# Gathering an expert's rows to 128 partitions with three of every four used, in a routed-experts layer in float32

## The reference, cut to what matters

```python
def hier_moe(x, ...):                       # x: normalized tokens, 1104 x 1024
    g = argmax(softmax(x @ w_rg + b_rg))    # one of 4 groups
    top_v, top_i = top_k(softmax(le_sel), 2)# two of the group's 8 experts
    expert = g * 8 + top_i                  # 2 of 32 experts for each token
    ...
    h = silu(xb @ w_eg[e]) * (xb @ w_eu[e]) # 1024 -> 512, twice
    return h @ w_ed[e]                      # 512 -> 1024
    ...                                     # times its gate, summed per token
```

## Time and profile before

| what | value |
| --- | --- |
| median of 3 runs | 1085.29 us (1083.37 to 1086.68) |
| the profiled execution's own time | 1084.18 us |
| its span, first to last instruction | 1082.3 us |
| mean granted TensorE clock | 0.974 of full |
| PE busy | 1015.9 us (94%) |
| DVE, ACT, POOL busy | 418.9, 241.0, 108.5 us |
| DMA, whole span | 262.34 MB, mean 242 GB/s |

### The profile page before, as it was taken

How to read it: one execution, slowest core, us unless ns; L and a number is a source line. 1 busy time by engine, 2 the same in 40 slices (tenths; PEclk the granted TensorE clock), 3 DMA queues, 4 the chain that set the end, 5 groups by cost and what they waited for, 6 DMA issues and landing times.

```text
span 1082.3 us, 33080 instructions
## 1 busy us (share of the span) xinstructions
PE 1015.9 (94%) x14746; PEld 827.0 (76%) x14746; DVE 418.9 (39%) x910; ACT 241.0 (22%) x509; POOL 108.5 (10%) x168
## 2 busy tenths in 40 slices
PE   8999999999999999989999999999999999999910
PEld 8786777768685959457888988889888898888810
DVE  2334443535262535362623323233232332323338
ACT  2442232323332322130110111111111111111123
POOL 0110101010100101001010111101111011110000
PEclk9999999999999999999999999999999999999965
DMA  9900010000000000629999999999999999999667
GB/s 331 347 19 40 1 40 0 39 0 39 0 39 20 18 39 1 274 115 332 402 404 398 406 405 399 412 401 406 404 395 408 392 406 394 387 402 384 272 226 297
DMA packets 53075, 262.34 MB, mean 242 GB/s; under 512 B 10301, under 2 KB 12925, under 8 KB 44842
## 3 DMA queue, kind: packets, MB, share of 16 engines
q1 hardware_dynamic: 43274, 234.20, 54.9%
q0 software_dynamic: 7168, 18.10, 5.0%
q10 hardware_dynamic: 2592, 9.44, 2.1%
HBM read 242.00 MB, written 26.80 MB: 248 GB/s over the span
## 4 chain that ended last, share of the span: by engine, by line
PE 91%; DVE 4%; DMA 2%; issue 1%; ACT 1%; SPq 0%; ACTq 0%; POOLq 0%; DVEq 0%
PE bank L1564 32%; PE bank L1279 18%; PE bank L1400 11%; PE bank L1575 10%; PE bank L1331 6%; PE bank L1581 6%; PE bank L1260 4%; DVE arena L1238 1%; PE bank L1380 1%; DVE arena L1236 1%; DVE arena L1244 1%; DMA arena<-in_w_in 1%; PE bank L1338 1%; PE bank L1397 1%; DMA arena<-pick_rows 1%
## 5 line engine op out<-in xcount | busy, mean ns | idle before, releaser
L1279 PE MATMUL bank<-xnT,arena 128*128 128x128 f32 x1728 | 201.0, 277 | 3.1 <-DMA arena<-in_w_in 1.8
L1279 PEld LDWEIGHTS bank<-xnT,arena 128*128 128x128 f32 x1728 | 196.8, 193 | 5.5 <-DVE sA L862 3.5
L1564 PEld LDWEIGHTS bank<-xnT,arena 128*64 128x64 f32 x4096 | 170.4, 137 | 6.5 <-issue 6.2
L1564 PEld LDWEIGHTS bank<-hnT,arena 128*64 128x64 f32 x4096 | 169.6, 137 | 7.5 <-issue 7.5
L1564 PE MATMUL bank<-hnT,arena 128*64 128x96 f32 x4096 | 173.0, 246 | 0.5 <-issue 0.5
L1564 PE MATMUL bank<-xnT,arena 128*64 128x96 f32 x4096 | 173.4, 247 | 0.0
L1120 DVE TENSOR_SCALAR mixT<-mixT 128x384 f32<-128x384 f32 x32 | 11.8, 368 | 319.5 <-ACT mixT L735 319.5
L1400 PE MATMUL bank<-arena,mixT 128*128 128x512 f32 x256 | 111.7, 593 | 0.0
L1400 PEld LDWEIGHTS bank<-arena,mixT 128*128 128x128 f32 x256 | 47.9, 190 | 57.2 <-issue 57.1
L1575 PE MATMUL bank<-arena,silu_r 128*32 128x384 f32 x768 | 85.8, 487 | 0.5 <-issue 0.5
L1581 PE MATMUL bank<-arena,osq 128*32 128x256 f32 x384 | 86.0, 380 | 0.0
(11 more groups left out here) (228 smaller groups left out, 975.1 us busy)
## 6 DMA issues: line engine op xcount, KB each, us to landing
arena<-in_w_eg SPq DMA_DIRECT2D x32, 2048.0 KB, 15.9
arena<-in_w_eu SPq DMA_DIRECT2D x32, 2048.0 KB, 16.3
arena<-in_w_ed SPq DMA_DIRECT2D x32, 2048.0 KB, 16.5
hn_rows<-hs ACTq DMA_DIRECT2D x18, 512.0 KB, 3.3
arena<-pick_rows SPq DMA_DIRECT2D x16, 512.0 KB, 10.8
arena<-in_w_in SPq DMA_DIRECT2D x3, 2048.0 KB, 11.8
arena<-in_w_out SPq DMA_DIRECT2D x1, 4096.0 KB, 13.5
out_y_prompt<-arena SPq DMA_DIRECT2D x8, 512.0 KB
```

The source lines that it names most:

```text
L1279: last = mm(out, w_in_sb[:, k, a:b], xnT[:, k, :], start=k == 0, stop=k == KD - 1)
L1564: last = mm(out[q * SW:(q + 1) * SW, n * BLOCK:(n + 1) * BLOCK], w[:, k, m * P + q * SW:m * P + (q + 1) * SW], rowsT[b][:, k, :], start=k ...
```

## The change

The rows of an expert are gathered to all 128 partitions: 32 groups of four partitions, of which the first three are used (lanes 0, 1, 2 of each group), 96 in all as before. A function `lane_of` gives the group and the lane of each rank: 16 consecutive ranks go to 16 different groups, over a table of two sets of groups. Two tables of ranks stand in the constants: `iota_lane` (128 wide, -1 at an unused lane) and `iota_block` (96 wide, the same ranks without the unused lanes). `at_rank`, `idx_f` and `idx_i` become 128 wide. The turn of the rows gives 128 columns in place of 96, and the copy out of PSUM reads the three used ones of each four, so `rowsT` has 96 columns as before, in the order of `iota_block`. The scatter still has 96 rows and needs an index without the unused lanes: three new DMAs on ScalarE's queue pick them from `idx_i` into `slot_idx`.

```diff
+LANE_GROUP = 4
+LANE_USED = LANE_GROUP * BLOCK // P
+LANE_GROUPS = P // LANE_GROUP
+LANE_SETS = ((0, 3, 5, 6, 9, 10, 12, 15), (1, 2, 4, 7, 8, 11, 13, 14))
+def lane_of(rank):
+    turn, n = divmod(rank, 16)
+    group = 16 * (n // 8) + LANE_SETS[turn % 2][n % 8]
+    return group, turn // 2
...
-    put("iota_block", (SPREAD * (np.arange(BLOCK) % RUN) + np.arange(BLOCK) // RUN)[None, :])
+    for rank in range(BLOCK):
+        group, n = lane_of(rank)
+        of_slot[LANE_USED * group + n] = rank
+        of_lane[LANE_GROUP * group + n] = rank
+    put("iota_block", of_slot[None, :])
+    put("iota_lane", of_lane[None, :])
...
-        at_rank = sb("at_rank", [P, PICKS, BLOCK])
+        at_rank = sb("at_rank", [P, PICKS, P])
-        idx_i = sb("idx_i", [BLOCK, NE], I32)
+        idx_i = sb("idx_i", [P, NE], I32)
+        slot_idx = sb("slot_idx", [BLOCK, NE], I32)
...
-        rows = [spare[0:BLOCK, 0:D], xs[0:BLOCK, :, :].rearrange("p k n -> p (k n)")]
+        rows = [spare[:, 0:D], xs[:, :, :].rearrange("p k n -> p (k n)")]
...
-                nc.gpsimd.tensor_copy(pick_idx[b][:, :], idx_i[:, bass.ds(e, 1)])...
+                nc.gpsimd.tensor_copy(pick_idx[b][:, :], slot_idx[:, bass.ds(e, 1)])...
+            pool.wait_ge(s["slot_idx_in"], 16 * LANE_USED)
             scatter(0, 0, first=True)
...
+            act.wait_ge(s["idx_ready"], 1)
+            for n in range(LANE_USED):
+                act.dma_start(slot_idx[n:BLOCK:LANE_USED, :], idx_i[n:P:LANE_GROUP, :]).then_inc(s["slot_idx_in"], 16)
             act.wait_ge(s["hn_stored"], 16 * PICKS * TILES)
...
-                    rank(V.tensor_scalar(at_rank[:, k, :], con("iota_block"), rk[:, k:k + 1], None, ALU.is_equal))
+                    rank(V.tensor_scalar(at_rank[:, k, :], con("iota_lane"), rk[:, k:k + 1], None, ALU.is_equal))
...
-                    V.tensor_tensor(rowsT[b][:, k, :], bank[half][:, 0:4 * BLOCK].rearrange("p (k n) -> p k n", n=BLOCK),
-                                    g_ffn[:, k].unsqueeze(2).to_broadcast([P, KD // 2, BLOCK]), ALU.mult)...
+                    V.tensor_tensor(rowsT[b][:, k, :].rearrange("p k (g n) -> p k g n", n=LANE_USED),
+                                    bank[half][:, :].rearrange("p (k g n) -> p k g n", g=LANE_GROUPS, n=LANE_GROUP)[:, :, :, 0:LANE_USED],
+                                    g_ffn[:, k].unsqueeze(2).unsqueeze(3).to_broadcast([P, KD // 2, LANE_GROUPS, LANE_USED]), ALU.mult)...
...
-                    last = mm(bank[7][0:BLOCK, 192:192 + NE], at_rank[:, k, :], M_tok[:, k, :], ...)
+                    last = mm(bank[7][:, 192:192 + NE], at_rank[:, k, :], M_tok[:, k, :], ...)
...
-                        last = turn(bank[half][:, k * BLOCK:(k + 1) * BLOCK], rows[b][:, c:c + P], BLOCK)
+                        last = turn(bank[half][:, k * P:(k + 1) * P], rows[b][:, c:c + P], P)
```

More of the change, by code:

```diff
@@ L67 @@
 NO_ROW = 4096
-SPREAD = 16
-RUN = BLOCK // SPREAD
+LANE_GROUP = 4
+LANE_USED = LANE_GROUP * BLOCK // P
+LANE_GROUPS = P // LANE_GROUP
+assert LANE_USED * LANE_GROUPS == BLOCK
+LANE_SETS = ((0, 3, 5, 6, 9, 10, 12, 15), (1, 2, 4, 7, 8, 11, 13, 14))
[3 more added lines that the diff above has]
+    return group, turn // 2
 BIG = 3.0e38
@@ L84 @@
 _WIDTHS = [("ident", P), ("keep", PAIRS * P), ("causal", P), ("before", P), ("count_fix", NG * META),
-           ("iota_block", BLOCK), ("iota_e", NE), ("first_g", GROUPS), ("first_e", PER_GROUP), ("pick", PICKS),
+           ("iota_block", BLOCK), ("iota_lane", P), ("iota_e", NE), ("first_g", GROUPS), ("first_e", PER_GROUP), ("pick", PICKS),
            ("valid", 1), ("block_edge", EXTRA_PER_E), ("iota_x", EXTRA), ("edge_x", EXTRA)]
@@ L107, in constants @@
     put("count_fix", np.concatenate([w / np.minimum(np.arange(META) + 1, w) for w in WINDOWS])[None, :])
-    put("iota_block", (SPREAD * (np.arange(BLOCK) % RUN) + np.arange(BLOCK) // RUN)[None, :])
+    of_slot, of_lane = np.full(BLOCK, -1.0), np.full(P, -1.0)
+    for rank in range(BLOCK):
[4 more added lines that the diff above has]
+    put("iota_lane", of_lane[None, :])
     put("iota_e", np.arange(NE)[None, :])
@@ L273, in build @@
         gate_all = sb("gate_all", [P, TILES, PICKS])
-        idx_f = sb("idx_f", [BLOCK, NE])
-        idx_i = sb("idx_i", [BLOCK, NE], I32)
+        idx_f = sb("idx_f", [P, NE])
+        idx_i = sb("idx_i", [P, NE], I32)
+        slot_idx = sb("slot_idx", [BLOCK, NE], I32)
         NP = TILES * PICKS
@@ L302, in build @@
         assert NH <= 3 * P
-        rows_idx = [sb(f"rows_idx{b}", [BLOCK, 1], I32) for b in range(2)]
+        rows_idx = [sb(f"rows_idx{b}", [P, 1], I32) for b in range(2)]
         pick_idx = [sb(f"pick_idx{b}", [BLOCK, 1], I32) for b in range(2)]
@@ L329, in build @@
             pe_eT pe_g pe_u2 pe_d sig_ready hid_ready eT_ready ye_ready row_idx_ready
-            x_tab_dve x_tab_pe x_idx_ready x_w x_rows x_pe x_dve x_act x_stored x_pool pick_idx_ready
+            x_tab_dve x_tab_pe x_idx_ready x_w x_rows x_pe x_dve x_act x_stored x_pool pick_idx_ready slot_idx_in
             fin_ready frstd_ready g_fin_in""").split()
@@ L509, in scatter @@
                     wait_parted(pool, ye_stored[b], 16 * t, s["parted"])
-                nc.gpsimd.tensor_copy(pick_idx[b][:, :], idx_i[:, bass.ds(e, 1)]).then_inc(s["pick_idx_ready"], 1)
+                nc.gpsimd.tensor_copy(pick_idx[b][:, :], slot_idx[:, bass.ds(e, 1)]).then_inc(s["pick_idx_ready"], 1)
                 wait_parted(pool, s["pick_idx_ready"], e + 1, s["parted"])
@@ L539, in _ @@
                     with pool.If(n < n_x):
-                        nc.gpsimd.tensor_copy(rows_idx[0][:, :], idx_xi[:, bass.ds(n, 1)]).then_inc(s["x_pool"], 1)
+                        nc.gpsimd.tensor_copy(rows_idx[0][0:BLOCK, :], idx_xi[:, bass.ds(n, 1)]).then_inc(s["x_pool"], 1)
                         wait_parted(pool, s["x_pool"], n + 1, s["parted"])
-                        nc.gpsimd.indirect_dma_start(rows[0], None, hn_dram, bass.IndirectOffsetOnAxis(ap=rows_idx[0][:, :], axis=0),
+                        nc.gpsimd.indirect_dma_start(rows[0][0:BLOCK, :], None, hn_dram, bass.IndirectOffsetOnAxis(ap=rows_idx[0][0:BLOCK, :], axis=0),
                                                      bounds_check=PICK_ROWS - 1, oob_is_err=False).then_inc(s["x_rows"], 16)
                         wait_parted(pool, s["x_act"], (1 + YE_STEPS) * (n + 1), s["parted"])
-                        nc.gpsimd.indirect_dma_start(y_dram, bass.IndirectOffsetOnAxis(ap=rows_idx[0][:, :], axis=0), ye[0], None,
+                        nc.gpsimd.indirect_dma_start(y_dram, bass.IndirectOffsetOnAxis(ap=rows_idx[0][0:BLOCK, :], axis=0), ye[0], None,
                                                      bounds_check=PICK_ROWS - 1, oob_is_err=False).then_inc(s["x_stored"], 16)
@@ L1010, in last_rank @@
                 rank.then(V.tensor_reduce(rk[:, :], prod[:, :, :], AX.X, ALU.add))
-                rank(V.tensor_scalar(at_rank[:, 0, :], con("iota_block"), rk[:, 0:1], None, ALU.is_equal))
-                V.tensor_scalar(at_rank[:, 1, :], con("iota_block"), rk[:, 1:2], None, ALU.is_equal).then_inc(s["onehot_ready"], 1)
+                rank(V.tensor_scalar(at_rank[:, 0, :], con("iota_lane"), rk[:, 0:1], None, ALU.is_equal))
+                V.tensor_scalar(at_rank[:, 1, :], con("iota_lane"), rk[:, 1:2], None, ALU.is_equal).then_inc(s["onehot_ready"], 1)
                 rank(V.tensor_tensor(prod_e[:, :, :], Mk, con("iota_e").unsqueeze(1).to_broadcast([P, PICKS, NE]), ALU.mult))
@@ L1019, in back_idx @@
                 rank(V.tensor_scalar(token[:, :], token[:, :], float(P), None, ALU.add))
-                V.tensor_tensor(idx_f[:, :], idx_f[:, :], bank[7][0:BLOCK, 192:192 + NE], ALU.add).then_inc(s["idx_added"], 1)
+                V.tensor_tensor(idx_f[:, :], idx_f[:, :], bank[7][:, 192:192 + NE], ALU.add).then_inc(s["idx_added"], 1)
             def body(i, first=False, last=False, second=False, third=False):
@@ L1096, in _ @@
             dve.wait_ge(s["pe_idx"], TILES)
-            V.tensor_tensor(idx_i[:, :], idx_f[:, :], bank[7][0:BLOCK, 192:192 + NE], ALU.add).then_inc(s["idx_ready"], 1)
+            V.tensor_tensor(idx_i[:, :], idx_f[:, :], bank[7][:, 192:192 + NE], ALU.add).then_inc(s["idx_ready"], 1)
             back_weights(j)
@@ L1112, in rows_turned @@
                     k = slice(half * KD // 2, (half + 1) * KD // 2)
-                    V.tensor_tensor(rowsT[b][:, k, :], bank[half][:, 0:4 * BLOCK].rearrange("p (k n) -> p k n", n=BLOCK),
-                                    g_ffn[:, k].unsqueeze(2).to_broadcast([P, KD // 2, BLOCK]), ALU.mult).then_inc(s["eT_ready"], 1)
+                    V.tensor_tensor(rowsT[b][:, k, :].rearrange("p k (g n) -> p k g n", n=LANE_USED),
+                                    bank[half][:, :].rearrange("p (k g n) -> p k g n", g=LANE_GROUPS, n=LANE_GROUP)[:, :, :, 0:LANE_USED],
```

(9 more changed lines are left out.)

## The result

| | before | after |
| --- | --- | --- |
| median, 10 runs each | 1086.78 us (1083.37 to 1089.32) | 1092.3 us (1089.51 to 1094.53) |
| ratio after to before | | 1.0055 (95%: 1.0042 to 1.0067), +6.0 us |
| span of the profiled execution | 1082.3 us | 1092.4 us |

The change makes the kernel slower by 0.55%, clear of the 0.3% that I had named. The prediction of 1087.1 us was too low, and so was the range, which ended at 1090.8. The profiled execution of before (1084.18 us) was quicker than nine of the ten runs, and that of after (1094.34 us) was the second slowest of ten, so the two spans differ by 10.1 us where the runs differ by 6.

What follows compares the result with a forecast made beforehand. TensorE was taken to bound the kernel, with no DMA in the expert stage's chain. Turn 1.9, marking product 0.3, passage 0.1 + 0.1 made +2.4 us, on 1084.7 giving 1087.1 us; range 1084.0 to 1090.8.

Steps and rivals of the forecast that it cites:

- What bounds the kernel: Expert stage: waits run over TensorE alone, 16.84 us from one up product to the next, no DMA in the chain.
- The turn: Eight transposes per expert, 128 columns for 96: 109 ns each for 101, 0.06 us an expert, +1.9 us; ceiling 7.2.
- rival C: Expert stage: the turn costs per column, 28 ns a transpose, 7.2 us in place of 1.9, total 1092.4 us; chance 0.06.
- The marking product: Front stage, L1449: stationary side grows from 96 to 128 columns, 8 ns a record over 9 tiles, +0.3 us (0 to 1.5).
- The passage: Last ranks to expert 0: wider at_rank +0.1 us; gather +0.1 us, more indices up to +0.4, more partitions down to -0.5.
- The copy, the three DMAs, the new wait, the constants: Expert 0's copy, other experts' covered copies, ScalarE's DMAs, GpSimd's wait and 64 KB more constants: each taken as cost 0.
- The base: Whole kernel before the change: 1084.7 us, the middle of four executions, on which the sum was put.
- Rival A: Late expert stage: empty gather entries put the DMA behind, TensorE waits 3.0 us for weights, total 1090.1 us; chance 0.13.
- Rival B: Expert stage: gathering to 128 partitions relieves the DMA, weights land in 16 us to the end, 1085.8 us; chance 0.17.

Runs made afterwards that it cites:

- The turn done twice: Kernel before, with the 8 transposes of each turn from expert 1 on done twice, the second over the first; ratio 1.0167, +18.1 us.
- the wide turn alone: Kernel before, with only the 128-column turn and a copy reading the first 96 of each 128; gather, ranks and scatter unchanged; ratio 1.0062, median 1091.89 us.
- the turn of 64 rows: Kernel before, with 7 of the 8 transposes of a turn cut to 64 rows and 64 columns; ratio 1.0005 against before.
- the turn of 96: The change, with turn and copy put back to 96 columns, rows on partitions 96 to 127 left out; ratio 0.9992 against before, median 1085.07 us.
- the plain order: The change, with before's order of ranks on the 128 partitions; ratio 1.0064 against before, median 1091.01 us.

## Why the prediction was wrong, step by step

**What bounds the kernel: right.** The chain of waits is TensorE's before and after, the step between experts holds everything, and a change of 0.2 us in it shows in full.

**The turn: mis-sized by 4.8 us (1.9 for 6.7), and the step that failed.** I divided the 0.81 us of a group of 96-column transposes by eight, got 101 ns, and compared it with 109 ns from a group of the front stage. The two groups have different neighbours. Ask for the same records one by one, by windows of 20 ns (each row begins with the start of the earliest transpose in its window). Before, in the expert stage:

```profile
605.94 0.30 PE L1260 MATMUL bank<-cst,xs 96*128 96x96 f32 x1
606.08 0.41 PE L1260 MATMUL bank<-cst,xs 96*128 96x96 f32 x3
606.16 0.41 PE L1260 MATMUL bank<-cst,xs 96*128 96x96 f32 x3
606.25 0.41 PE L1260 MATMUL bank<-cst,xs 96*128 96x96 f32 x3
606.33 0.41 PE L1260 MATMUL bank<-cst,xs 96*128 96x96 f32 x3
...
606.58 0.25 PE L1260 MATMUL bank<-cst,xs 96*128 96x96 f32 x1
606.75 0.52 PE L1575 MATMUL bank<-arena,osq 128*32 128x384 f32 x3
```

From 606.08 to 606.58 there are six steps, 83 ns each. The first takes 0.14 us (605.94 to 606.08) and the last 0.17 us (606.58 to 606.75), which I put down to the array going over from and to matmuls of another size; that reading was not tested by itself. The front stage is in line with it: behind the group of eight in the earlier trace rows stand two more 128 x 128 transposes, of `k_dec`, and from the second of them to the 64 x 64 products that follow, the step is 0.20 us and not 0.11, in all nine tiles. After:

```profile
610.39 0.33 PE L1285 MATMUL bank<-cst,xs 128*128 128x128 f32 x1
610.55 0.38 PE L1285 MATMUL bank<-cst,xs 128*128 128x128 f32 x2
610.66 0.38 PE L1285 MATMUL bank<-cst,xs 128*128 128x128 f32 x2
610.77 0.38 PE L1285 MATMUL bank<-cst,xs 128*128 128x128 f32 x2
...
611.21 0.27 PE L1285 MATMUL bank<-cst,xs 128*128 128x128 f32 x1
611.41 0.52 PE L1600 MATMUL bank<-arena,osq 128*32 128x384 f32 x3
```

110 ns each inside (610.55 to 611.21), with 0.16 and 0.20 us at the ends. The front stage's group has 109 to 110 ns throughout, and full-size instructions stand on both sides of it. So the row that I took was right for the new pace and the row that I held against it was not the old pace: 109 - 83 = 26 ns a transpose, and not 8. The 26 ns are the ceiling that I had worked out (28 ns, 7.2 us) and made rival C at a chance of 0.06. The turn done twice shows the split of pace and ends in its own kernel, the wide turn alone shows the sum. What no run separates is the cause inside a transpose: with its moving columns the partitions that it contracts over grew too, from 96 to 128. The Trainium skill (FP8 and Floating Point Precision, "TensorE Precision Notes") gives true float32 four passes; for 128 columns at 2.4 GHz that makes an estimate of 213 ns, and the trace has 110. So the trace disagrees with four passes for a transpose, and disagreed before; what I drew from that, that columns hardly cost, didn't follow. Two cycles a column at 2.4 GHz, also an estimate, make 107 ns for 128 columns and 80 for 96, each 3 ns under the measured pace; but for 64 columns they make 53 ns, and the turn of 64 rows has 62, so this fits only the upper two.

**The marking product: 0.6 us for 0.3.** 20 ns a record, between my bounds of 0 and 43, in the seven tiles where projections follow it; in the eighth TensorE waits behind it, and the step is 0.95 us before and after. Between the pooling products of the first and the last tile the kernels with before's tables took 397.5 to 397.6 us, those with the change's 398.1 (the turn of 96), 398.6 (the plain order) and 399.2 (the change). The turn of 96 has just the 0.6 us. The other 0.5 and 1.0 us stand in one step, from the pooling product of the third tile to that of the fourth (52.06 and 52.60 us for 51.56); in the change's chain most of it is a pause of 0.69 us at 152.96 us, marked "issue". The turn of 96 has the same tables and no such pause, so it is not shown to be theirs.

**The passage: about 0.5 us the other way.** The gather's step took 3.70, 3.89 and 3.95 us in the three profiled executions with 128 partitions and 4.14 to 4.42 in the six with 96. I had put +0.1 and allowed for -0.5. The issue on GpSimd grew from 1.13 to 1.18 us, not by a third.

**The copy, the three DMAs, the new wait, the constants: right.** The three DMAs are issued from 488.4 to 489.6 us, beside a first gather that lands sooner than before's. The copy's median on `xnT` is 556 ns before and after, though it now reads pieces of three:

```profile
L1137 DVE TENSOR_TENSOR xnT<-bank,g_ffn x32: 545/556/558, 494.3 to 1004.2; 128x384 f32<-128x384 f32 x32
```

**The base.** I put the sum on 1084.7 us, from four executions; ten runs have before at 1086.78. Of the 5.2 us between 1087.1 and the measured 1092.3, 2.1 are this base, and the rest is the change: 5.5 us between the medians, 6.0 by the ratio, for 2.4. The parts are 6.7 us from the turn and 0.6 from the tables, less 0.5 from the passage, 6.8 us on paper; the runs say 6.0 (4.6 to 7.3). The rest of the 10 us between the two profiles is chance as far as can be seen: 0.7 us in the first weights' step (9.68 for 8.96), 0.9 from there to the first tile, with the clock at its lower level for 6.8 us there in place of 3.4, the 1.0 us of the step between two tiles, and 1.1 us in the first up product.

**Rival A: wrong.** The empty entries built no backlog; q0 took 8.0% of the engines with 1478 packets where it had taken 9.6% with 1344. (That an empty entry moves nothing is so by the queue's count of bytes and not by the HBM's, as the last section shows.) **Rival B: half right.** The relief is real and is worth nothing. The Trainium skill's port map (SBUF — State Buffer, "Door 1: The DMA port swizzle") speaks for it, and the weights' landing agrees in its direction: at the same step of TensorE, gate weights land after 10.4 us with 128 partitions and after 14.4 to 15.9 us in three profiles with 96. The gathers themselves land after 10.1 to 12.0 us from 600 us on where before's took 7.9 to 13.3, no quicker on the whole, so which step of the DMA got cheaper is not shown. **Rival C: what happened.**

## What to carry to other kernels

Two groups of the same instruction can be compared only by the steps inside them; the ends of a group belong to its neighbours, and in a group of eight they were 0.3 of 0.8 us. When a bound from another row gives nearly four times the value that you take, look at single records before you give it 6%. And relieving a queue that is full but that nobody waits for gains no time, so it must not cost anything on the engine that sets the pace: here it cost 0.2 us an expert.

## What the runs showed of the hardware

The entries that a gather's bounds check skips are read from HBM all the same, by the count of bytes. The HBM line of the page, of the change and then of the wide turn alone, which gathers as before:

```profile
HBM read 246.26 MB, written 26.80 MB: 250 GB/s over the span
```

```profile
HBM read 242.00 MB, written 26.80 MB: 247 GB/s over the span
```

The change has 32 gathers x 32 more empty entries; at 4096 bytes each that is 4.19 MB, and 0.07 MB are the wider constants (64 KB): together the 4.26 MB of difference. The queue's own count of bytes stays at 18.10 MB in both. Here it cost no time: the turn of 96 has the same 246.26 MB and before's time.

A change of a transpose's size inside a group (96 to 64 rows) cost about 0.12 us (0.23 and 0.12 us where a group of one size has 0.14 and 0.08), as much as the shorter transposes behind it saved.
